# Ending stages with a semaphore-only barrier, and moving expert slots inside sampled attention

## The reference

```python
n  = rmsnorm(x);  qa,ka,va, qb,fb,ib,gb, gate_a,gate_b = split(n @ w_in)
oa = diff_attention(qa, ka, va)       # sampled tokens: 512 cached keys and values each, by a page table
ob = hgrn2(qb, fb, ib) * silu(gb)     # recurrent state; sampled tokens: one update of a cached state
h  = x + (sigmoid(gate_a)*(oa @ w_a) + sigmoid(gate_b)*(ob @ w_b)) @ w_out
# PEER: each token picks 8 heads x 16 = 128 of 16384 experts
idx, w = top16_of_product_keys(rmsnorm(h) @ w_query)
a  = gelu(einsum('td,tkd->tk', rmsnorm(h), expert_u[idx]))
h  = h + einsum('tk,tkd->td', w * a, expert_v[idx]);   y = rmsnorm(h)
```

## Time and profile before

| | us |
|---|---|
| three runs, median (lowest to highest) | 3852.43 (3852.02 to 3865.66) |
| the profiled execution, its own time | 3850.09 |
| span of its trace, first to last instruction | 3848.4 |
| TensorE busy in the span | 2857.7 (74%) |
| VectorE / ScalarE / GpSimd busy | 2471.6 / 927.3 / 1009.0 |
| mean granted TensorE clock | 0.86 of full |

### The profile page before, as it was taken

The page is one execution under the profiler, slowest core; times in us unless marked ns, Lnnn a source line. Parts: engine busy times, 40 slices in busy tenths (PEclk is TensorE's granted clock), DMA queues, the critical chain, the costliest instruction groups (busy, mean ns, idle before and its releaser), DMA issues. The chain is left out here.

```text
span 3848.4 us, 30261 instructions
## 1 busy us (share of the span) xinstructions
PE 2857.7 (74%) x9486; PEld 1603.9 (42%) x9486; DVE 2471.6 (64%) x5235; ACT 927.3 (24%) x2189; POOL 1009.0 (26%) x746
## 2 busy tenths in 40 slices
PE   6749378525962794445399508699999999999998
PEld 5436344323531442322154306545555555555554
DVE  2231746774859666877267589766666666676666
ACT  1220111632311114611132115411112111121111
POOL 0000024122420342235233100033333333333332
PEclk9769689667986897766699758899999999999999
DMA  6234299556970896546689405499999999999996
GB/s 215 74 112 142 72 380 379 178 198 245 405 299 18 344 371 223 206 178 212 231 332 376 145 14 204 173 408 405 396 390 398 405 414 394 397 399 395 399 403 252
DMA packets 249838, 1075.90 MB, mean 280 GB/s; under 512 B 25336, under 2 KB 87800, under 8 KB 162240
## 3 DMA queue, kind: packets, MB, share of 16 engines
q0 software_dynamic: 99872, 704.82, 46.7%
q1 hardware_dynamic: 149808, 369.17, 25.5%
HBM read 1008.35 MB, written 65.55 MB: 279 GB/s over the span
## 5 line engine op out<-in xcount | busy, mean ns | idle before, releaser
L1565 POOL DMA_INDIRECT arena<-in_experts,arena x640 | 918.1, 1434 | 2020.6 <-DVE arena L1608 2001.8
L1608 DVE SCALAR_TENSOR_TENSOR arena<-arena 128x1024 f32<-128x1024 f32 x640 | 819.1, 1280 | 103.9 <-ACT arena L1586 103.7
L1644 DVE CUSTOM_DVE_ANT_0 arena<-arena 128x1024 f32<-128x1024 f32 x640 | 780.6, 1220 | 74.7 <-DMA arena<-in_experts,arena 61.7
L2206 PE MATMUL d_s_ps<-arena 128*128 128x384 f32 x2048 | 686.9, 487 | 22.2 <-DMA arena<-in_ut 22.2
L2215 PE MATMUL d_acc<-arena 128*128 128x512 f32 x1536 | 679.4, 592 | 0.0
L2206 PEld LDWEIGHTS d_s_ps<-arena 128*128 128x128 f32 x2048 | 386.9, 189 | 328.0 <-issue 80.1
L2215 PEld LDWEIGHTS d_acc<-arena 128*128 128x128 f32 x1536 | 291.2, 190 | 341.3 <-issue 307.2
L1584 ACT ACTIVATE arena<-arena 128x1 f32<-128x1 f32 x640 | 129.2, 202 | 971.0 <-DVE arena L1644 970.4
L2259 DVE TENSOR_TENSOR arena<-arena 128x384 f32<-128x384 f32 x128 | 71.7, 560 | 443.9 <-ACT arena L2237 431.6
L1586 ACT ACTIVATE arena<-arena 128x1 f32<-128x1 f32 x640 | 188.4, 294 | 20.7
L2237 ACT ACTIVATE arena<-d_s_ps 128x384 f32<-128x384 f32 x128 | 63.0, 492 | 441.1 <-PE d_s_ps L2206 441.1
(11 more groups left out here) (446 smaller groups left out, 3290.3 us busy)
## 6 DMA issues: line engine op xcount, KB each, us to landing
arena<-in_ut SPq DMA_DIRECT2D x128, 512.0 KB, 13.0
arena<-in_vd SPq DMA_DIRECT2D x128, 512.0 KB, 10.2
arena<-in_w_t SPq DMA_DIRECT2D x96, 512.0 KB, 8.0
wd_scratch<-arena SPq DMA_DIRECT2D x12, 2048.0 KB, 7.0
arena<-wd_scratch SPq DMA_DIRECT2D x16, 1536.0 KB, 29.4
arena<-in_w_n SPq DMA_DIRECT2D x9, 2048.0 KB, 7.8
arena<-in_w_out SPq DMA_DIRECT2D x24, 512.0 KB, 8.4
arena<-in_w_query SPq DMA_DIRECT2D x24, 512.0 KB, 3.5
```

The source lines that it names most:

```text
L1565: pool.indirect_dma_start(out=c["ring"][:, s0 % RING, :], out_offset=None, in_=self.io["experts"], in_offset=bass.IndirectOffsetOnAxis(ap= ...
L1608: dve.scalar_tensor_tensor(out=h, in0=c["ring"][:, r, D:2 * D], scalar=c["coef"][:, r:r + 1], in1=h, op0=ALU.mult, op1=ALU.add).then_inc(s ...
L1644: dve.tensor_tensor_reduce(out=u, in0=u, in1=self.entry(i)["n2"], scale=1.0, scalar=0.0, op0=ALU.mult, op1=ALU.add, accum_out=c["dots"][:, ...
L2206: last = nc.tensor.matmul(s_ps[j % 2][:, 0:DN], us[j % NU][:, k, :], n2t[:, :, k, :], start=(k == 0), stop=(k == KD - 1))
```

## The change

2. `Side` knows three kinds of points: `HEAD = (0, 1)`, then the even spread, then `TAIL = (2, 1)`. `SHARES` gets two more numbers, the slots hosted at the head and at the tail. Only three stages have other numbers than 0: `hgrn_out` of `b_` (head 2) and of `c_` (head 3), `attend_sample` (tail 2). All shares stay the same.
3. In `attend_sample` GpSimd asks for all 16 sets of cached rows first and for expert rows after them; the score loop hosts no slot; VectorE hosts 10 slots after the weights are laid out and 2 at its very end; TensorE makes the states' product after the values of token 5 and no longer ahead of the weights.
4. In `hgrn_out` ScalarE does the head's gelus before it waits for the gate.

```diff
+HEAD, TAIL = (0, 1), (2, 1)
...
-        block = st.enter_context(nc.Block())
+        block = st.enter_context(nc.Block(no_gpsimd_drain=True))
...
@@ attend_sample
-                side.pool(n, 2 * NS)
-            side.pool(1, 1)
+            side.pool(*TAIL)
...
+            def states():
+                pe.wait_ge(qz_ready, NS)
+                pe.wait_ge(new_ready, NS)
+                for h in range(H):
+                    for b in range(NS):
+                        last = nc.tensor.matmul(so_ps[:, h, :], q_z[:, h, b, :], s0[:, b, h, :],
+                                                start=(b == 0), stop=(b == NS - 1))
+                last.then_inc(so_done, 1)
...
                 last.then_inc(v_used, 1)
+                if b == NRING - 1:
+                    states()
...
                 nc.scalar.copy(v_sb[:], v_ps[:]).then_inc(v_copied, 1)
-                side.act(b + 1, 2 * NS)
+                if b == 0:
+                    side.act(*HEAD)
...
                                  ACT.Copy, scale=c["subln"][:, 0:1]).then_inc(oat_stored, 1)
+            side.act(*TAIL)
...
                 v.tensor_tensor(s0[:, b], s0[:, b], kv[:], ALU.add).then_inc(new_ready, 1)
-                side.dve(b + 1, 2 * NS)
...
                 last.then_inc(wz_ready, 1) if b == NS - 1 else link(last)
+            side.dve(1, 1)
             dve.wait_ge(so_done, 1)
             link(v.tensor_copy(o_all[0:NS, len(g.tiles) - 1], so_ps[:]))
-            side.dve(1, 1)
             dve.wait_ge(v_used, NS)
...
             v.tensor_tensor(o_sb[:], o_sb[:], bcast(o_ss[:], [NS, H, DV], 2), ALU.mult).then_inc(on_ready, 1)
+            side.dve(*TAIL)
@@ hgrn_out
         def _(act):
+            side.act(*HEAD)
             act.wait_ge(gate_landed, 16 * (1 + g.sampled))
             nc.scalar.activation(flat(gate), flat(gate), ACT.Silu).then_inc(silu_done, 1)
-            side.act(1, 2)
...
-            side.dve(1, 2)
+            side.dve(*HEAD)
@@ Side
     def due(self, done, total):
-        if self.last and done == total:
+        if self.last and done >= total:
             return self.end
-        return self.begun + self.share * done // total
+        if done > total:
+            return self.given
+        return self.begun + self.head + (self.share - self.head - self.tail) * done // total
...
+          ("b_", hgrn_out): (4, 2, False, 2, 0),
+          ("c_", attend_sample): (12, 5, False, 0, 2), ("c_", hgrn_out): (6, 5, False, 3, 0),
```

More of the change, by code:

```diff
@@ L1069, in _ @@
             last.then_inc(s_turned, 1)
[L1070 to L1076, removed]
             pe.wait_ge(pr_ready, 1)
@@ L1518, in stage @@
     def stage(self, build, g):
-        share, self.open, self.last = SHARES[g.name, build]
+        share, self.open, self.last, self.head, self.tail = SHARES[g.name, build]
         self.begun = self.given
@@ L1523, in stage @@
         self.share = self.given - self.begun
+        assert self.head + self.tail <= self.share or self.last
     def due(self, done, total):
-        if self.last and done == total:
+        if self.last and done >= total:
             return self.end
-        return self.begun + self.share * done // total
+        if done > total:
+            return self.given
+        return self.begun + self.head + (self.share - self.head - self.tail) * done // total
     def where(self, b):
@@ L1569, in pool @@
         self.at["pool"] = max(self.at["pool"], to)
-        if self.last and done == total and not self.closed["pool"]:
+        if self.last and done >= total and not self.closed["pool"]:
             self.closed["pool"] = True
@@ L2345, in program @@
         side.sems.end()
[L2348 to L2353, removed]
+SHARES = {("b_", project): (46, 2, False, 0, 0), ("b_", attend_prompt): (14, 2, False, 0, 0),
+          ("b_", hgrn): (12, 2, False, 0, 0), ("b_", hgrn_out): (4, 2, False, 2, 0),
+          ("b_", merge): (54, 2, False, 0, 0), ("b_", route): (0, 2, False, 0, 0),
+          ("c_", project): (58, 5, False, 0, 0), ("c_", attend_prompt): (20, 5, False, 0, 0),
+          ("c_", hgrn): (12, 5, False, 0, 0), ("c_", attend_sample): (12, 5, False, 0, 2),
+          ("c_", hgrn_out): (6, 5, False, 3, 0), ("c_", merge): (54, 5, False, 0, 0),
+          ("c_", route): (0, 5, False, 0, 0), ("c_", spread): (0, 5, False, 0, 0),
+          ("c_", dense): (640, 5, True, 0, 0)}
 def lay_out(inputs):
```

35 lines of the change are left out of this document (25 added, 10 removed).

## The result

The changed kernel took 3792.44 us (median of four runs, 3787.81 to 3800.29), the kernel before 3852.22 (3847.51 to 3865.66) on the same chip: ratio 0.984, 95% interval 0.9823 to 0.9856. That is 60 us faster; I had forecast 3859, no change that can be told, and 3792 lies outside the range that I gave. The profiled execution took 3794.72 us with a span of 3792.9, so the two traces differ by 55.5 us.

What follows compares the result with a forecast made beforehand. TensorE bounds the last 1355 us (dense), untouched, so the change's worth lies in the 2493 us before and stage ends. Terms 0 + 11.3 + 0 - 4.0 = +7.3 on 3852.43 give 3859.7; predicted 3859 us, range 3840 to 3870.

Steps and rivals of the forecast that it cites:

- the rival's "Against": Argument against L160 and L161 not waiting for rows: the L161 drain and the one ending route had equal price, 0.034 us.
- The bound of -71.7: Ends of project, hgrn and merge, both passes: the most that removing GpSimd's block-end drain could give, 71.7 us.
- My +7.3 us: Whole kernel: sum of all terms, 0 + 11.3 + 0 - 4.0, slower by 7.3 us.
- The six ends, 0 us: Ends of project, hgrn and merge, where GpSimd comes last: L160's drain takes over the wait, gain 0, bounds 0 and -71.7.
- Hidden drains, +11.3: Ends where other engines hide GpSimd's drain: behind the barrier it costs 0.8 us at five ends, 7.3 at dense.
- `attend_sample`, 0: Stage attend_sample: what the products gain, the drain at the end takes; 0 us, bounds -11.1 and +0.3.
- The products ending 12.9 us earlier: In attend_sample: value products end at 1839.1, where VectorE goes on from them at 1852.0 today, 12.9 us earlier.
- The drain taking it back: End of attend_sample: two last slots release GpSimd's last request at 1849.4, its drain ends at 1860.8, against 1860.5 today.
- `hgrn_out`, -4.0: Stage hgrn_out: gelus first spare VectorE's waits, 3.0 us in c_ and 1.0 in b_; bounds -4.3 and 0.
- The drain is really gone: Rival: L160 and L161 don't wait for rows; 3766 us, or 3790 if half of four ends comes back; chance 0.12.
- The mark that I had named: Sign in the changed trace: L160 drains staying near 0.1 us would mean L160 and L161 don't wait for rows.
- The full price of 7.3 us at every end: Rival: each drain has a fixed price, five hidden ends pay 36.5 us in place of 4.0; 3892 us, chance 0.09.

Runs made afterwards that it cites:

- fourth experiment: Kernel before with one unused semaphore cleared by GpSimd (resetting DRAIN and clear) ahead of each block's own plain drain: 3807.48 us, ratio 0.9884.
- third experiment: Kernel after with one plain GpSimd drain added in Stage.end ahead of the semaphore clear, behind the barrier: 3858.89 us, ratio 1.002.
- second experiment: Kernel after with GpSimd's drain back at every block's end, so only the new orders in attend_sample and hgrn_out remain: 3850.0 us, ratio 0.9978.
- last experiment: Kernel after with ScalarE's old order in hgrn_out, gate and silu ahead of the head's gelus: 3802.13 us, ratio 0.9858.
- fifth to seventh experiment: Kernel after, no rows asked ahead in merge: 3776.89 us; also none at hgrn c_ and hgrn_out ends: 3760.38; also project's first request awaiting weights: 3762.39.

## Why the prediction was wrong

**The step that failed.** "The same instruction, with nothing to wait for, has the same price; so I take it that the drain at L160, the first to meet the rows in flight, does the waiting that the block's end does now." show two drains with nothing in flight; that they are equal there says nothing of what each does when rows are in flight, and neither of them is L160's, the resetting one. Nor was its price equal, as the rival's "Against" has it: L160's own row (in the section on the result), in the trace all along, has 0.077 to 0.110 us, against the 0.034 of L161's.

The bound of -71.7 stood beside it, and I took the other end. The runs show that the plain DRAIN waits for landings in either place (7.9 us ahead of the barrier and 8.3 behind it at the end of `hgrn` c_) and the resetting one in neither (1.2 and 1.0 us there; fourth experiment and kernel after). With a plain drain in that place the kernel takes 3858.89 us, 0.07 to 0.33% (3 to 13 us) more than the kernel before beside it. My +7.3 us is a forecast of that kernel; that 3859 hits it to the us is luck, since the kernel before took 3856.3 there.

**The two kinds of DRAIN.** At the end of `hgrn` c_ the plain DRAIN of the kernel before ended 6.7 us after the last request was written (1688.0 + 0.9 = 1688.9, against 1687.7 + 7.9 = 1695.6), and the plain one of the third experiment took 8.3 us at the same end. The resetting one in the changed kernel ended 0.1 us after the last request was written, 11.7 us before the landing. I had let the plain one speak for both.

**The six ends, 0 us.** Measured 61.7. Of the bound of 71.7 GpSimd's own writing stays: some 1 us at four ends, 6.2 at `merge` c_. I had also read the drain as over 0.5 us after the landing. That holds after the 12 requests of `hgrn`; after the 60 of `project` c_ it was 2.5 us, from a landing at 1470.8 + 14.5 = 1485.3 to the drain's end at 1470.6 + 17.2 = 1487.8 (source view of the kernel before):

```profile
L1565 POOL DMA_INDIRECT arena<-in_experts,arena x1: 936/936/936, 1470.8 to 1470.8; - x1
...
DMA to landing us min/median/max: 14.5/14.5/14.5
```

Worked out from the traces for all six ends, some 10 us of the 71.7 lie behind the last landing.

**Hidden drains, +11.3.** As prices of plain drains they were right: 1.2, 0.4, 1.7, 0.5 and 0.7 us at the five ends and 7.3 at `dense` in the third experiment, 4.5 + 7.3 = 11.8. In the changed kernel the one plain drain of a stage's end, L163's, stands behind the resetting one and takes 0.05 us at most, so the term is 0.

**`attend_sample`, 0.** The term has two halves. The products ending 12.9 us earlier: 16.2 from the first key product on, less 3.8 by which that product is later, so 12.4. That this is near 12.9 is luck: the products with the states' took 36.3 us and not the 41.6 that I had worked out, they began 1.9 us later behind the first key product than I had them, and the 3.8 I had left out. The drain taking it back: right with a plain drain (second experiment), wrong with the resetting one. Measured -9.1; SyncE's store of the rows (its DRAIN at 1813.8) and the last two requests (written by 1814.6) set the end, with the clear at 1814.7.

**`hgrn_out`, -4.0.** Measured +1.3 and -0.3. With every drain kept, the case that I had forecast, the new order gives 1.1 in `b_` and 2.2 in `c_` (second experiment), 3.3 for my 4.0. In the changed kernel the order is worth more, 4.0 and 2.9 (last experiment), but it meets what I had left out, because I had the rows landed at the stage's start: in `b_` the gate comes beside rows in flight, and the silu 3.5 us later. In `c_` ScalarE waits 9.8 us for the first store and not 5.2; with the new order it waits 8.0 in the second experiment too, where every drain is kept, so rows let through by the missing drain explain 2 us of this at most, and the cause of the rest stays open.

**The rivals.** "The drain is really gone" was the case, with a chance of 0.12. Its 3790, with half of four ends given back, is 2 us from the measured time, in part by luck: the ends gave 10 us less than it has, `attend_sample` 2 and `hgrn_out` 5 less, while the give-back in the other bodies was nearer 15 than 24. The mark that I had named, L160's drains near 0.1 us, came at one of the six ends alone (0.08); at four they took 1.0 and at one 6.2, the time of writing requests. It is that they end ahead of the landing which tells this rival from the others. The full price of 7.3 us at every end is ruled out even for plain drains by the third experiment's 0.4 to 1.7.

## What to carry to other kernels

Two drains that cost the same with nothing in flight are not yet the same drain: where a wait is said to move to another instruction, look for one row in which that instruction meets the condition, and if the trace has none, leave both ends in the forecast with real chances. A wait for transfers at a stage's end may go where every reader waits for its own landing; but here the transfers then met the next stage's first loads (in `route` of `b_` the first product came 8.3 us after the start in place of 3.9), so ask for them only when the next stage's loads are in. That second step was worth about half as much again here (3792 to 3760).

## What the runs showed of the hardware

- GpSimd's plain DRAIN, with rows in flight, ended after their landing, and the longer after it the more requests had been made since the last drain: 0.5 us with 12 (`hgrn` c_), 2.3 with 54 (`project` b_, `merge` b_), 2.5 with 60 (`project` c_), each the same to 0.05 us in the kernel before and in the second and third experiments. The resetting one, ahead of the clear, ended 0.1 us after they were written (1.0 us in all, against 8 to 17 for the plain one, at four ends), and a plain one behind it and its clear took 0.05 us with rows in flight.
- With everything landed a plain DRAIN still took 0.4 us after 4 requests, 1.7 after 20 and 7.3 after 347 (third experiment). What it does in that time no run shows.
- One request in `merge` of `c_` took 9.9 us in every kernel that asked for rows ahead there, always the same one; in the three runs that hold them back (fifth to seventh experiment) no request takes over 3.0 us. Its cause stays open.
